# First projections of a four-stage kernel: seven block products in place of eight, in units of 1024 tokens

## The reference, cut to what matters

```python
h = rms_norm(x, norm_g)
dx = token_shift(h) - h
x_r, x_w, x_k, x_v, x_a, x_g = (h + dx * mu[i] for i in range(6))
r = x_r @ w_in[:, 0:1024]
k = x_k @ w_in[:, 1024:2048]
v = x_v @ w_in[:, 2048:3072]
g = jax.nn.silu(x_g @ w_in[:, 3072:4096])
# later: kk = heads(k * k_k), the low-rank projections of x_w and x_a, the recurrence, w_out
```

## Time and profile before

| | |
|---|---|
| runs of the kernel | 3111.95, 3114.89, 3125.24 us; median 3114.89 |
| profiled execution, span from first to last instruction | 3120.0 us |
| busy: TensorE, VectorE, ScalarE, GpSimd | 2897.5, 1605.3, 1080.2, 619.7 us |
| mean granted clock of TensorE | 0.970 |
| first projections, from the first to the last matmul | 39.7 to 754.7 us |
| three groups of projection matmuls (L331), busy | 402.1, 399.6, 399.5 us |

### The profile page before, as it was taken

One profiled execution on the slowest core, in us unless ns is written; L12 is line 12 of the kernel. 1 busy time (PEld: TensorE's weight loads), 2 busy tenths in 40 slices (PEclk: granted clock), 3 DMA queues, 4 the chain that ended last, 5 costly groups with the idle time before them and its releaser, 6 DMA issues. The chain is left out here.

```text
span 3120.0 us, 78648 instructions
## 1 busy us (share of the span) xinstructions
PE 2897.5 (93%) x35058; PEld 2391.3 (77%) x35058; DVE 1605.3 (51%) x2628; ACT 1080.2 (35%) x2001; POOL 619.7 (20%) x417
## 2 busy tenths in 40 slices
PE   7999999999878888888889999999999999999899
PEld 4887888887467787777777778888777897777677
DVE  5533242433177677677764662222377204777762
ACT  4223332322635445454453441000222113556310
POOL 5522222210023232232321120000000001332320
PEclk9999999999979899899998999999999999999999
DMA  5123331211833232332316763111111226225472
GB/s 173 61 78 115 108 105 48 95 48 53 260 103 112 64 105 77 92 106 70 105 37 179 223 180 74 34 41 41 41 61 61 88 89 229 74 88 181 154 245 85
DMA packets 344272, 326.20 MB, mean 105 GB/s; under 512 B 14159, under 2 KB 258255, under 8 KB 343296
## 3 DMA queue, kind: packets, MB, share of 16 engines
q1 hardware_dynamic: 315344, 261.72, 27.6%
q10 hardware_dynamic: 24480, 47.21, 4.3%
q0 software_dynamic: 4112, 12.25, 1.5%
HBM read 203.18 MB, written 122.64 MB: 104 GB/s over the span
## 5 line engine op out<-in xcount | busy, mean ns | idle before, releaser
L331 PE MATMUL pj_ps<-pj_x_hi,pj_w_hi 128*128 128x512 f32 x1024 | 402.1, 393 | 10.6 <-DVE pj_w_lo L280 5.8
L331 PE MATMUL pj_ps<-pj_x_hi,pj_w_lo 128*128 128x512 f32 x1024 | 399.6, 390 | 0.0
L331 PE MATMUL pj_ps<-pj_x_lo,pj_w_hi 128*128 128x512 f32 x1024 | 399.5, 390 | 0.0
L1924 PE MATMUL dm_ps<-h_hi,dm_w_hi 128*128 128x512 f32 x896 | 279.5, 393 | 0.0
L1924 PE MATMUL dm_ps<-h_lo,dm_w_hi 128*128 128x512 f32 x896 | 275.9, 389 | 0.0
L1924 PE MATMUL dm_ps<-h_hi,dm_w_lo 128*128 128x512 f32 x896 | 275.8, 389 | 0.0
L221 POOL TENSOR_TENSOR pj_x<-h 128x512 f32<-128x512 f32 x128 | 166.7, 1303 | 485.5 <-DVE pj_x_lo L275 436.2
L275 DVE TENSOR_TENSOR pj_x_lo<-pj_x,pj_x_hi 128x512 fp32r<-128x512 f32 x128 | 91.4, 714 | 319.3 <-ACT pj_x_hi L350 319.1
L331 PEld LDWEIGHTS pj_ps<-pj_x_hi,pj_w_hi 128*128 128x128 f32 x1024 | 192.9, 188 | 54.6 <-DVE pj_w_lo L280 8.4
L331 PEld LDWEIGHTS pj_ps<-pj_x_lo,pj_w_hi 128*128 128x128 f32 x1024 | 193.1, 189 | 40.9 <-issue 1.0
L331 PEld LDWEIGHTS pj_ps<-pj_x_hi,pj_w_lo 128*128 128x128 f32 x1024 | 192.8, 188 | 40.4
(11 more groups left out here) (260 smaller groups left out, 6053.9 us busy)
## 6 DMA issues: line engine op xcount, KB each, us to landing
proj<-pj_out ACTq DMA_DIRECT2D x128, 256.0 KB, 2.5
pj_w<-w_in SPq DMA_DIRECT2D x32, 512.0 KB, 4.2
proj<-lr_out SPq DMA_DIRECT2D x32, 512.0 KB, 5.0
dm_w<-w_out SPq DMA_DIRECT2D x32, 512.0 KB, 5.3
dm_w<-w_in SPq DMA_DIRECT2D x32, 512.0 KB, 4.9
partial<-wa_ob SPq DMA_DIRECT2D x48, 264.0 KB, 2.2
mo_part<-partial SPq DMA_DIRECT2D x16, 792.0 KB, 8.6
wa_vt<-v_rows SPq DMA_DIRECT2D x44, 260.0 KB, 3.2
```

The lines of the kernel that those rows point to most:

```text
L331: mm = pe.matmul(ps[i][:], wp, xp, start=k == 0 and m == 0, stop=k == KT - 1 and m == len(parts) - 1)
L1924: last = pe.matmul(PS[:, 2 * i + b, :], wp, hp[:, k, t0:t0 + 512], start=k == 0 and m == 0, stop=k == KT - 1 and m == len(parts) - 1)
```

## The change

The four products become Strassen's scheme in the form with seven products and fifteen additions. A projection is cut into two units of 1024 tokens, eight units (`g`) in all. In a unit, the weight matrix is four blocks a11, a12, a21, a22 of 512x512 and the input four blocks of 512 channels x 512 tokens. Each product p is four channel slices k ("tiles" n = 28 g + ..., 224 in all), and the slice is the outer loop: one tile is 4 column blocks x 3 matmuls into four banks. Products 1, 5, 3 and 7, 6, 4 and 2 use the eight banks in turn; 2, 6 and 3 add to what is in their bank already.

Splits are made per tile into rings of five (`DEEP`): 224 casts and 224 rests for inputs, and as many for weights. The inputs and weights of a product are formed in place by GpSimd. `hi` parts are on ScalarE; rests of x are on VectorE but for 62 of them on GpSimd (`on_pool`). The blend is h * (1 - mu) on ScalarE (`kept`) plus the shifted h * mu on VectorE, instead of a difference on GpSimd. Banks are emptied by ScalarE after products 1, 7 and 2, and by VectorE sums after 6, 5, 4, 3. The roots of the last three token blocks lie in SBUF (`side`). Weights are loaded per unit by 1 MB, stores are of 1 MB and issued by SyncE, the second key output goes through `side`.

The diff, cut ("..." stands for what is left out); it is some 300 lines removed and 700 added.

```diff
-    w_lo = sb("w_lo", [128, KT, KT, 128], F32R)
-    w_hi = sb("w_hi", [128, KT, KT, 128], F32R)
...
+QT = T // 4
+HK = KT // 2
+DEEP = 5
+UNITS = 8
+STEP = HK
+UNIT = 7 * STEP
+ALL = UNITS * UNIT
...
+    w_hi, w_lo = (sb(n, [128, DEEP, QT], F32R) for n in ("w_hi", "w_lo"))
+    x_hi, x_lo = (sb(n, [128, DEEP, QT], F32R) for n in ("x_hi", "x_lo"))
+    u3, u2, out, side = (sb(n, block) for n in ("u3", "u2", "out", "side"))
...
+    def products_of(g):
+        return (1, 2, 7, 6, 5, 4, 3) if g == 0 else (1, 7, 2, 6, 5, 4, 3)
+    def on_pool(n):
+        r = (n - 4) % UNIT
+        return n >= 18 and (14 <= r < 18 or 22 <= r < 26)
...
@@ gpsimd @@
+        def form_x(g, p, k):
+            X = [x[:, k, :] for x in xs]
+            if p == 7:
...
+                made = pool.tensor_tensor(X[3], X[2], X[3], ALU.subtract)
+            elif p == 6:
+                x_split(pool, g, 7, k)
+                pool.wait_ge(s_tx, tx_at(g, 7, k))
+                made = pool.tensor_tensor(X[3], X[3], X[0], ALU.add)
...
+        def form_w(g, p, k):
...
+                made = pool.tensor_tensor(a21, a11, a21, ALU.subtract)
...
+        def less_u3(g, j):
...
+            pool.tensor_tensor(u2[:, j, :], u3[:, j, :], u2[:, j, :], ALU.subtract).then_inc(s_u2, 1)
+        def forms(n):
+            if 5 <= n < 9:
+                form_x(0, 7, n - 5)
+            for at in () if 6 <= n < 9 else (2 * n - 6, 2 * n - 5) if 9 <= n < 12 else (n + 6,):
...
+                if p in X_FORMS and (g, p) != (0, 7):
+                    form_x(g, p, k)
+                if p in W_FORMS:
+                    form_w(g, p, k)
...
@@ vector @@
+        def body(n):
+            total(dve, n)
...
+            for at in prepared(n):
+                if not on_pool(at):
+                    low_x(at)
+                low_w(at)
...
+            if n >= 9 and (at := blended(n - 1)) and at[0]:
+                for name in at[1]:
+                    blend(at[0], name, at[2])
+            silu(dve, n - 2)
...
+        def scale(b, kk):
+            by = ps[0][:] if b == 0 else side[:, ROOT[b], :]
...
@@ tensor @@
+        def body(n):
+            g, p, k = tile_of(n)
...
+            await_x_lo(pe, n)
+            pe.wait_ge(s_w_lo, n + 1)
+            at = n % DEEP
+            for j in range(4):
+                if k == 0:
+                    free(g, p, j)
...
+                J = slice(128 * j, 128 * j + 128)
+                parts = product_parts(w_hi[:, at, J], w_lo[:, at, J], x_hi[:, at, :], x_lo[:, at, :])
+                for m, (wp, xp) in enumerate(parts):
+                    first = p not in (2, 6, 3) and k == 0 and m == 0
+                    mm = pe.matmul(bank(g, p, j)[:], wp, xp, start=first, stop=k == HK - 1 and m == len(parts) - 1,
+                                   skip_group_check=True)
...
@@ scalar @@
+        def high_x(n):
+            g, p, k = tile_of(n)
+            if n >= DEEP:
+                act.wait_ge(s_mm, n - DEEP + 1)
...
+    def gate(act, g, p, j, at):
+        if g // 2 == 1:
+            m = output_at(g, p, 2)
+            if m:
+                act.wait_ge(s_st_side, 16 * m)
...
@@ low-rank stage @@
     def gpsimd(pool):
         before_gpsimd(pool)
-        inputs_read(pool, 3)
+        stored(pool)
         pool.memset(rb[:], NEG).then_inc(s_neg, 1)
...
         before_vector(dve, beside)
+        rings_read(dve)
         for b in range(NB):
...
             if b == 0:
+                last_sums(dve)
```

More of the change, by code:

```diff
@@ L145, in projection_programs @@
+    ones, eps, keep = sb("ones", [128, 128]), sb("eps", [128, 1]), sb("keep", [128, 4 * KT])
+    ps = [c.enter_context(nc.psum_tensor(f"pj_ps{i}", [128, QT], F32)) for i in range(8)]
+    return raw, xs, w_hi, w_lo, x_hi, x_lo, u3, u2, out, side, ones, eps, keep, ps
 def projection_programs(sems, buffers, src, h, gain, vec, w_in, proj):
-    QT = T // 4
-    x_lo, x_hi, x, w, w_lo, w_hi, out_sb, scaled, sq, ones, eps, ps, var = buffers
+    raw, xs, w_hi, w_lo, x_hi, x_lo, u3, u2, out, side, ones, eps, keep, ps = buffers
@@ L150, in sem @@
     def sem(n):
         return sems.new(f"pj_{n}")
[L153 to L158, removed]
@@ L159, in projection_programs @@
-    s_mm, s_ps_free, s_sig = sem("mm"), sem("ps_free"), sem("sig")
-    s_out, s_scaled = [sem(f"out{i}") for i in range(2)], sem("scaled")
+    s_first = [sem(f"h0{i}") for i in range(HK)]
+    s_block = [[sem(f"h1{i}") for i in range(2)], [sem("h2")], [sem("h3")]]
+    s_ones, s_keep, s_square, s_summed, s_part, s_total, s_log, s_normed = (sem(n) for n in (
+        "ones", "keep", "square", "summed", "part", "total", "log", "normed"))
+    s_y, s_blend, s_tx, s_tw, s_x_hi, s_x_lo, s_x_less, s_w_hi, s_w_lo = (sem(n) for n in (
+        "y", "blend", "tx", "tw", "x_hi", "x_lo", "x_less", "w_hi", "w_lo"))
@@ new lines, in gpsimd @@
+        for b in (2, 3):
+            pool.wait_ge(s_normed, 3 * (b - 1))
+            pool.dma_start(h[:, :, tokens(b)], src[:, :, QT * b:QT * (b + 1)]).then_inc(s_block[b - 1][0], 16)
+            for k in (1, 2) if b == 2 else range(3, KT):
+                part(1, k)
+        for n in range(2, ALL):
+            forms(n)
+            for at in prepared(n):
+                if on_pool(at):
+                    low(at)
+            if 5 <= n < 9:
+                for k in (1, 2) if n == 5 else (3, 4) if n == 6 else (5, 6) if n == 7 else (7,):
+                    part(2, k)
+            g, r = divmod(n, UNIT)
+            if 4 * STEP + 1 <= r < 5 * STEP + 1:
+                less_u3(g, r - 4 * STEP - 1)
@@ L444, in projection_programs @@
-    return sync, gpsimd, vector, tensor, scalar, stored, inputs_read, sums_read, spare
+        high_w(0)
+        kept(0, "b11", 0)
+        high_w(1)
+        kept(0, "b11", 1)
+        for k in range(HK):
+            high_x(k)
+            if k + 2 < HK:
+                kept(0, "b11", k + 2)
+                high_w(k + 2)
+        for k in range(HK):
+            square(1, 2 * k)
+            square(1, 2 * k + 1)
+            kept(0, "b21", k)
+        for n in range(ALL):
+            body(n)
```

765 lines of the change are left out of this document (514 added, 251 removed).

## The result

| | before | after |
|---|---|---|
| runs, us | 3111.18 to 3125.24, median 3113.42 (4) | 3185.78 to 3202.15, median 3191.28 (4) |
| ratio, 95% interval | | 1.0242 [1.0215, 1.0269] |
| profiled span, us | 3120.0 | 3186.8 |
| granted clock of TensorE, mean | 0.970 | 0.952 |
| end of the last projection matmul, us | 754.7 | 820.4 |

What follows compares the result with a forecast made beforehand. SBUF access shared by VectorE and GpSimd bounds it: 732 us, 762 at 0.96 use; stage end 19 + 762 + 4 + 4 + 3 = 792 against 754.7, +43 with passage, 3158 us timed; 8 in 10: 3065 to 3235.

Steps and rivals of the forecast that it cites:

- TensorE's saving, 87 us: First projections: 2688 matmuls, 384 fewer at 0.2267 us each, save 87 us and leave 609 us.
- Which resource: First projections: the SBUF access that VectorE and GpSimd share becomes the new bound, 732 us against TensorE's 609.
- TensorE's waits were to be named by the rests: Sign for 100 to 700 us: TensorE's waits named by rests of x and w on VectorE and GpSimd.
- The holds, 1.12 and 0.55: Colliding two-input operations: GpSimd's holds the shared access 1.12 us, VectorE's rest, gate product or sum of squares 0.55.
- VectorE's rest of 121.32 behind L244: Timeline before the change: this rest takes 1.75 us for 0.69, as if begun 1.14 after GpSimd's L244 began undisturbed.
- 0.96 of use: Whole projection stage: share of time in which either engine holds the access, turning 732 us into 762.
- Start: +4 (0 to +10): First 25 us of the projections: a chain with ScalarE between leaves the access half empty, +4 us.
- Gates of the key units, +4: Key units: scaled copies wait on ScalarE for the previous output's `side` store, four waits, +4 us (0 to +25).
- Rival 4, whole durations: Projections: each operation keeps the other out for its whole duration, 871 us of access, 3267 us timed; chance 10%.
- Passage, +6: From last projection product to low-rank stage: line matmuls about 20.5 us after the last matmul, before 14.6; +6 (0 to +12).
- TensorE's clock: Projections: no rival, since a granted clock of 0.94 throughout would make 609 us into 648, still under 762.
- 732 us: Projections: summed holds of the shared access, 408 us for GpSimd, 234 and 90 for VectorE.

Runs made afterwards that it cites:

- e3: The changed kernel with all forms of inputs and weights, the u3 - u2 differences and all rests on VectorE, 350 operations moved off GpSimd: 3093.48 us, ratio 0.9930.
- e9: The changed kernel with each of GpSimd's 256 forms replaced by two fills that read nothing, combinations left out: 3071.81 us, ratio 0.9850.
- e5: The changed kernel without the hi x lo matmuls of the first projections, 1792 of 2688 left: 3177.59 us, ratio 1.0188.
- e1: The changed kernel with the 62 rests of x that GpSimd makes moved to VectorE: 3177.73 us, ratio 1.0202.
- e2: The changed kernel with the 128 forms of the weights on VectorE in place of GpSimd: 3147.03 us, ratio 1.0099.
- e10: The changed kernel with each of GpSimd's 256 forms replaced by a copy of its first operand, combinations left out: 3087.42 us, ratio 0.9904.

## Why the prediction was right in its mechanism and short in its size

- **TensorE's saving, 87 us:** right, and not to be had. The first matmul came at 24.8 (forecast: about 24). Undisturbed, in e3, TensorE takes 78 to 83 us for each of the five middle units, against 76 for the matmuls.
- **Which resource:** right. Least of a form 1.26 to 1.28, mean 1.65 to 1.74 (forecast 1.6 to 1.9); rests with a mean of 1.17 and 1.22 (forecast over 1.0); PSUM sums at 0.68; TensorE busy 87% from 100 to 700 us (75% in the first 100 of them, 86 to 93% behind that), forecast 80 to 88. One sign was wrong: TensorE's waits were to be named by the rests, and those end 10.9 us of them; the sums out of PSUM, queued behind the rests, end 79.5.
- **The holds, 1.12 and 0.55:** right to a few hundredths. A pair takes 1.69 us, where they make 1.67. The forecast's own row, VectorE's rest of 121.32 behind L244, gives 1.14 and not 1.12; over 364 operations that is 7 us. The forecast's 85 us a unit at 0.96 of use is 88.7, with 1.14 it is 89.6; the five middle units took 89.7.
- **What was mis-sized, 28 us of stage end (820.4, forecast 792):** mostly the use outside those units. The step that failed is "Start: +4 (0 to +10)", with the term of 0.96 that was set for the whole stage. For the first unit the forecast has 85 and 34 for the sums of squares and scales of the token blocks (14 x 1.12, 7 x 0.55, 24 x 0.59), so 119/0.96 + 4 = 128; it took 139.5. For the seventh, 85 + 9 for sixteen gate products, over 0.96, so 98; it took 111.7. These two are 25 of the 28. The first unit is a chain as much as a load: in e9, where forms disturb nobody, it still takes 116.8 us (44.5 to 161.3), where 336 matmuls want 76. TensorE's totals of the squares wait 12.3 us for ScalarE and 3.5 for VectorE there; in the change (L578) 13.7 and 11.6. In such waits the access stands free, and what is lost there isn't made good later, since the rest runs at its limit. The sixth and seventh units, columns as above:

```profile
543.46:633.76 90.30, 80.58 (x338) 64.80 (x337) 89.10 (x81) 47.69 (x85) 72.99 (x45) 0.96 0.27 94
633.76:745.47 111.71, 90.99 (x353) 70.92 (x351) 108.96 (x103) 57.21 (x102) 80.33 (x49) 0.87 0.21 76
```

The seventh has 353 matmuls in it where the sixth has 338: ScalarE's copy of 745.47, which marks its end, waited 2.79 us for a store, so some 3 us (15 matmuls) belong to the eighth. The seventh is longer than the sixth in every run, by 21.4 us in the change, 20.4 in e5, 12.7 in e3 and 8.8 in e9, so by most where forms collide. What made it some 10 us longer than its load was not tested.
- **Gates of the key units, +4:** the waits are there, 17.6 us in four for the `side` store, but they cost nothing that can be seen. The two units took 95.8 and 88.5 us, and the one behind them 83.9; by the count of matmuls in these stretches, 352, 338 and 324, it is the marks that are late. Together they are 268.1 us for as many matmuls as three stretches of 90.3 hold (270.9 us).
- **Rival 4, whole durations:** wrong as the rows had it. By it a pair would take 1.28 + 0.69 = 1.97, measured 1.69. The turns are real; what the whole durations claim too much is 0.28 us a pair.
- **Passage, +6:** 4.6. VectorE's eight rests come first, as forecast, then sums and gate products to 831.4, then the store, and only then the tables. The rows of all engines in order of time, for the earlier trace rows:

```profile
820.46 4.92 DVE L946 TENSOR_TENSOR lr_h_low<-h,lr_h_hi 128x513 fp32r<-128x513 f32 x8 [1.58 <-PE pj_ps L598]
...
835.61 0.10 POOL L910 MEMSET lr_rb<- 33x8 f32 x1 [26.76 <-DMA proj<-pj_u]
...
839.63 3.98 PE L987 MATMUL lr_up<-lr_hot,lr_rb 33*8 33x383 f32 x6 [6.92 <-DMA lr_hot<-onehot]
```

- **TensorE's clock:** as forecast no rival, though it fell further than the 0.94 allowed for. The granted clock was 0.85 where TensorE was busy 75% and 1.00 in e3 from 200 to 600 us, but in e5 from 200 to 600 us, with a third less to do and the clock at 0.83 to 0.88, TensorE still stood idle for a quarter of the time or more.

The expectations for e1 and e2 priced moves by A's full hold. e1 and e2 show less: 14 of 34 and 44 of 70 us. My reading, which no run separates: the bound is VectorE's queue with its waits for the access in it, rather than the access alone. From 200 to 700 us VectorE is busy 492.78 us and GpSimd 403.30, and that queue also holds the sums out of PSUM, which need no turn and hide a part of GpSimd's hold. What an operation on GpSimd costs that queue is then, by estimate, what its move gained and the 0.60 that it costs on VectorE: 0.82 us in e1, 0.94 in e2, 0.88 in e3, in place of 1.12.

## What to carry to other kernels

When a change takes work from the busiest engine and gives it to two that share an access to memory, add up what the two *hold* together, not what each does alone: 732 us stood behind two loads of 466 and 500. An engine with slack is no place for such work if each operation there costs its neighbour more than the neighbour would need to do it itself: here 1.12 us held on GpSimd, or 0.8 to 0.9 as the moves priced it, against 0.60 on VectorE. A mean use taken from a stretch at its limit holds for the middle of a stage; the first unit of the stage and any unit with other work want a sum of their own, with their chain.

## What the runs showed of the hardware that was not expected

- A GpSimd copy of a contiguous 128x512 tile (one input in SBUF) takes 0.61 us at the least and keeps VectorE's two-input operation out for only about 0.45 us (e10); an operation with two inputs does so for 1.12 to 1.15. A fill takes 0.53 and keeps it out not at all (e9).
- A VectorE sum out of PSUM, placed before a colliding operation, hides a part of GpSimd's hold: the rest behind it takes 1.17 to 1.19 in place of 1.75 to 1.79.
- VectorE alone fits 159 operations of 128x512 into 100 us, one per 0.63, while both engines together make 137 in the same stretch of the change.
